# Feed forward up projections of a four layer decoder by one level of Strassen's algorithm, with sums of weights on GpSimd

## The reference

```python
def rms_norm(x, g, eps=RMS_EPS):
    xf = x.astype(jnp.float32)
    y = xf * lax.rsqrt(jnp.mean(xf * xf, axis=-1, keepdims=True) + eps)
    return (y * g.astype(jnp.float32)).astype(x.dtype)

def swiglu(x, w_in, w_out):
    gate, up = jnp.split(x @ w_in, 2, axis=-1)
    return (jax.nn.silu(gate) * up) @ w_out

# per layer:
x = x + mixed
x = x + swiglu(rms_norm(x, W['norm_ffn'][i]), W['ffn_w_in'][i], W['ffn_w_out'][i])
```

## Time and profile before

| | us |
|---|---|
| median of 3 runs | 3497.66 |
| lowest and highest | 3496.62, 3501.85 |
| the profiled execution | 3500.84 |
| its span, first to last instruction | 3499.2 |
| TensorE matmul busy | 3332.0 |
| VectorE busy | 1887.7 |
| ScalarE busy | 1054.7 |
| GpSimd busy | 130.9 |

### The profile page before, as it was taken

How to read it: one execution, slowest core, us unless ns; L and a number is a source line. 1 busy time by engine, 2 the same in 40 slices (tenths; PEclk the granted TensorE clock), 3 DMA queues, 4 the chain that set the end, 5 groups by cost and what they waited for, 6 DMA issues and landing times.

```text
span 3499.2 us, 77068 instructions
## 1 busy us (share of the span) xinstructions
PE 3332.0 (95%) x32788; PEld 3168.7 (91%) x32788; DVE 1887.7 (54%) x2957; ACT 1054.7 (30%) x1674; POOL 130.9 (4%) x247
## 2 busy tenths in 40 slices
PE   8999999998998999988989898899999999899997
PEld 7998899998777999988978777799999999799997
DVE  6667643445655543447457666553344666654343
ACT  3222322223554322223333333332223222232221
POOL 0000000001221000000000000000000000000000
PEclk9999999999999999999999899999999999999998
DMA  3222222223343222221200000122222222122221
GB/s 123 86 80 73 68 85 89 86 94 99 124 126 92 86 95 81 93 89 56 79 17 11 19 11 14 53 87 97 80 97 79 76 78 77 58 91 92 83 91 67
DMA packets 103584, 269.40 MB, mean 77 GB/s; under 512 B 12690, under 2 KB 45714, under 8 KB 103010
## 3 DMA queue, kind: packets, MB, share of 16 engines
q1 hardware_dynamic: 90338, 228.94, 20.1%
q0 software_dynamic: 13056, 37.64, 3.2%
HBM read 248.01 MB, written 18.52 MB: 76 GB/s over the span
## 4 chain that ended last, share of the span: by engine, by line
PE 79%; DVE 11%; DVEq 3%; ACT 3%; issue 2%; SPq 0%; DMA 0%; ACTq 0%
PE ps L559 63%; PE ps L985 4%; PE ps L660 3%; PE ps L977 1%; PE ps L691 1%; PE ps L707 1%; PE ps L1081 1%; DVE cell L2166 1%; DVE arena_r L1873 1%; DVEq L2429 1%; DVE arena L2033 1%; PE ps L685 1%; DVE rstd L1852 1%; DVEq L2165 0%; DVE h L2163 0%
## 5 line engine op out<-in xcount | busy, mean ns | idle before, releaser
L559 PE MATMUL ps<-arena_r 128*128 128x272 f32 x11136 | 1500.5, 293 | 67.4 <-DVE arena_r L2297 21.2
L559 PEld LDWEIGHTS ps<-arena_r 128*128 128x128 f32 x11136 | 1434.4, 191 | 109.0 <-issue 60.7
L559 PE MATMUL ps<-hb_r,arena_r 128*128 128x272 f32 x8448 | 1060.7, 288 | 0.4 <-DVE hb_r L1866 0.4
L559 PEld LDWEIGHTS ps<-hb_r,arena_r 128*128 128x128 f32 x8448 | 1058.5, 188 | 1.1 <-DVE hb_r L1866 0.8
L1368 ACT ACTIVATE arena_r<-ring 128x1024 fp32r<-128x1024 f32 (+1 forms) x240 | 275.3, 1147 | 913.0 <-PE ps L559 913.0
L1892 DVE TENSOR_TENSOR arena_r<-ring,arena_r 128x1024 fp32r<-128x1024 f32 (+1 forms) x240 | 319.6, 1332 | 142.9 <-ACT arena_r L1368 142.9
L1932 DVE TENSOR_TENSOR arena<-ps,rstd 128x544 f32<-128x544 f32 x88 | 63.7, 724 | 292.9 <-PE ps L559 292.9
L1953 DVE TENSOR_TENSOR x<-x,ps 128x544 f32<-128x544 f32 x64 | 46.2, 721 | 293.5 <-PE ps L559 293.5
L1350 ACT ACTIVATE arena_r<-ring 128x1024 fp32r<-128x1024 f32 x80 | 84.6, 1057 | 229.7 <-PE ps L559 224.8
L660 PE MATMUL ps<-arena 128*128 128x128 f32 x1024 | 140.0, 281 | 9.2 <-DVE arena L1996 6.8
L660 PEld LDWEIGHTS ps<-arena 128*128 128x128 f32 x1024 | 128.8, 195 | 13.1 <-issue 7.3
(11 more groups left out here) (387 smaller groups left out, 3099.6 us busy)
## 6 DMA issues: line engine op xcount, KB each, us to landing
ring<-in_w_up SPq DMA_DIRECT2D x176, 512.0 KB, 3.5
ring<-in_w_mix SPq DMA_DIRECT2D x112, 512.0 KB, 3.5
ring<-in_w_down SPq DMA_DIRECT2D x64, 704.0 KB, 4.0
arena<-in_hg_s POOLq DMA_DIRECT2D x16, 512.0 KB, 3.7
out_hg_so<-arena POOLq DMA_DIRECT2D x16, 512.0 KB, 2.9
ring<-in_w_hgout SPq DMA_DIRECT2D x16, 512.0 KB, 3.5
arena<-in_cache_k SPq DMA_DIRECT2D x128, 64.0 KB, 1.9
arena<-in_cache_v POOLq DMA_DIRECT2D x128, 64.0 KB, 2.2
```

The costliest lines, as they stand in the source:

```text
L559: mm = pe.matmul(PS[:, 2 * a + hf, 0:HALF], part[:, ws], rhs[:, o:o + HALF], start=start and n == 0, stop=stop and n == 2)
```

## The change

The gate and linear units of a block are taken as a 2 x 2 matrix of weight blocks: A11 and A12 are the first and second 512 rows of the gate unit, A21 and A22 those of the linear unit. The activations are a 2 x 2 matrix too: first and second half of the features by first and second half of the tokens. Instead of eight products of such blocks there are seven (`NPROD`): A11, S2, S1, S3, A12, A22, S4, in this order. Each has 4 chunks of 3 terms on 272 columns, 12 matmuls. S1 = A21 + A22, S2 = S1 - A11, S3 = A21 - A11 and S4 = S2 - A12 (`sum1` to `sum4`). GpSimd makes the four sums for each pair, from the weights in `ring`, into `ff_s`. The activations' sums T (`ff_t`, `ff_t2` to `ff_t4`, `ff_n1`) are made once for each layer, by GpSimd and VectorE, and split in high and low parts by ScalarE and VectorE.

The seven operands of a pair are split one by one: seven high copies on ScalarE and seven low parts on VectorE, 512 columns each, in five rotating buffers (`ff_operand`, `ff_freed`). The results are combined as the products end. ScalarE copies the product A11 (`ff_e1`); VectorE makes u2, u3 and the four quarters of gate and linear on 272 columns each; `rstd` is multiplied into the two quarters of gate by VectorE and into the whole of linear by GpSimd (`ff_lr`). silu, the product of gate and linear and the split of the result come one pair later. TensorE waits inside a pair three times: before S3 until u2 has read the bank of S2, before A12 until the copy of A11 is made, and before S4 until the second half of linear has read the bank of S1.

21 of the 22 pairs of a layer go this way (`FF_PAIRS` is 10 and 11); the first pair of a layer keeps its 96 matmuls, while the activations' sums are made. The first down unit begins with chunks 8 and 9, and its weights are split in three pieces. SyncE's loads are written out, and the slots of a pair become free when its seven low parts are made. Everything outside the feed forward stays.

```diff
+        NPROD = 7
+        FF_PAIRS = (FU - 1, FU)
...
+        A11, S2, S1, S3, A12, A22, S4 = range(NPROD)
+        WHICH_S = {S1: 0, S2: 1, S3: 2, S4: 3}
+        WHICH_T = {S2: 0, S1: 1, S3: 2, A22: 3}
+        ACCS = (0, 1, 2, 1, 0, 3, 2)
...
+                def pair(s, i, par, first=False):
+                    n0 = NPROD * par
+                    bank = 4 * ((par + 1 - s) % 2)
+                    for k in range(NPROD):
+                        pe.wait_ge(S("ff_wl"), i * (2 * NPROD) + (ff_splits(layer, s) + n0 + k + 1))
+                        if k == S3:
+                            pe.wait_ge(S("ff_u"), i * 6 + (3 * ff_pairs(layer, s) + 3 * par + 1))
+                        if k == A12:
+                            pe.wait_ge(S("ff_e1"), i * 2 + (ff_pairs(layer, s) + par + 1))
+                        if k == S4:
+                            pe.wait_ge(S("ff_u"), i * 6 + (3 * ff_pairs(layer, s) + 3 * par + 2))
+                        wh_, wl_ = ff_operand(s, n0 + k)
+                        begin = k in (A11, S2, S1, A22)
...
+                            hi, lo = token_side(k, c)
+                            for m, (weights, rhs) in enumerate(((wh_, hi), (wh_, lo), (wl_, hi))):
+                                mm = pe.matmul(PS[:, bank + ACCS[k], 0:HALF], weights[:, ws], rhs,
+                                               start=begin and c == 0 and m == 0, stop=c == KC // 2 - 1 and m == 2,
+                                               skip_group_check=True)
+                                if k == S4 and c == KC // 2 - 1 and m == 1:
+                                    mm.then_inc(S("unit_done"), 2)
+                        mm.then_inc(S("ff_p"), 1)
...
+                def first_down(s):
+                    pe.wait_ge(S("ff_x"), 2 * KC * layer + KC * s + 1)
+                    pe.wait_ge(S("ff_g"), FC * layer + FU * s + FU - 1)
+                    for n, c in enumerate((8, 9, 0, 1, 2, 3, 4, 5, 6, 7, 10)):
+                        if n in (0, 2, 6):
+                            pe.wait_ge(S("ff_wl"), ff_downs(layer, s) + (0, 2, 6).index(n) + 1)
+                        pe.wait_ge(S("ff_al"), FC * layer + FU * s + c + 1)
+                        mm = unit_block(2, 0, SLOT, c, ff_ah, ff_al, n == 0, n == FU - 1)
...
-                        for g in range(2):
-                            pe.wait_ge(S("ff_wl"), i * 4 + (unit0 + 2 * par + g + 1))
-                            if begin and not s and par and g:
-                                pe.wait_ge(S("norm_rms"), nth(name) + 1)
-                            first = begin and not s and par == 0
-                            product(2 * par + g, g, ff_hh, ff_hl, KC, "ff_hl" if first and not g else None, KC * layer)
...
+                def pair(s, i, par, begin=False, end=False):
+                    n0 = NPROD * par
+                    weights(s, i, n0 + 4, not (begin and par == 0))
+                    if not (s and begin and par == 0):
+                        silu(s, i, par)
+                    first_product(s, i, par)
...
+                    weights(s, i, n0 + 5)
+                    weights(s, i, n0 + 6)
+                    if not (s and begin and par == 0):
+                        high_a(s, i, par)
+                    if not end:
+                        for k in range(4):
+                            n = n0 + NPROD + k
+                            weights(s, i + n // (2 * NPROD), n % (2 * NPROD))
...
+                    weights(s, i, n0 + 4)
+                    if first and not s:
+                        low_t(3, lambda c: ff_hh[:, c * NT + HALF:(c + 1) * NT],
+                              lambda c: ff_hl[:, c * NT + HALF:(c + 1) * NT], ff_t4)
+                    weights(s, i, n0 + 5)
+                    made(S2)
+                    dve.wait_ge(S("ff_e1"), i * 2 + (ff_pairs(layer, s) + par + 1))
+                    dve.tensor_tensor(ff_u2, b, ff_e1, ALU.add).then_inc(S("ff_u"), 1)
+                    weights(s, i, n0 + 6)
+                    if not (first and s):
+                        glu(s, i, par, not first)
+                    ahead(0)
+                    if not (first and s):
+                        low_a(s, i, par)
+                    made(S3)
+                    dve.tensor_tensor(ff_u3, b, ff_e1, ALU.add)
+                    dve.drain()
+                    dve.tensor_tensor(lin[:, HALF:NT], ff_u3, c, ALU.subtract).then_inc(S("ff_u"), 1)
+                    ahead(1)
+                    made(A12)
+                    dve.tensor_tensor(gate[:, 0:HALF], a, rstd[:, 0:HALF], ALU.mult)
+                    ahead(2)
+                    made(A22)
+                    dve.tensor_tensor(lin[:, 0:HALF], ff_u3, d, ALU.add).then_inc(S("ff_u"), 1)
+                    ahead(3)
+                    made(S4)
+                    dve.tensor_tensor(gate[:, HALF:NT], ff_u2, c, ALU.subtract)
+                    dve.drain()
+                    dve.tensor_tensor(gate[:, HALF:NT], gate[:, HALF:NT], rstd[:, HALF:NT], ALU.mult).then_inc(S("ff_g"), 1)
...
-                        if not first:
-                            ff_rest(layer, i, n + 2, width)
-                        dve.wait_ge(S("unit_done"), i * 4 + (base + n + 2))
-                        dve.tensor_tensor(halves(ff_lin[par]), acc(2 * par + 1), halves(rstd[:, :]), ALU.mult)
-                        if not first:
-                            ff_rest(layer, i, n + 3, width)
-                        dve.drain()
-                        dve.wait_ge(S("ff_silu"), i * 2 + (par + 1 + block0))
-                        dve.tensor_tensor(ff_gate[par], ff_gate[par], ff_lin[par], ALU.mult).then_inc(S("ff_glu"), 1)
...
+                def sum1(s, n):
+                    a11, a12, a21, a22 = raw(s, n)
+                    pool.tensor_tensor(ff_s[0], a21, a22, ALU.add).then_inc(S("ff_s"), 1)
...
+                    pool.tensor_tensor(ff_s[1], ff_s[0], a11, ALU.subtract).then_inc(S("ff_s"), 1)
...
+                    pool.tensor_tensor(ff_s[2], a21, a11, ALU.subtract).then_inc(S("ff_s"), 1)
...
+                    pool.tensor_tensor(ff_s[3], ff_s[1], a12, ALU.subtract).then_inc(S("ff_s"), 1)
+                def pair(s, i, par, end=False):
+                    if not end:
+                        nx, n = par + 1, (par + 1) % 2 * NPROD
+                        arrived(s, i + nx // 2, n)
+                        split(s, i, par, S1)
+                        sum1(s, n)
+                        made(s, i, nx, 1)
+                        sum2(s, n)
+                        split(s, i, par, S3)
+                        sum3(s, n)
+                        made(s, i, nx, 3)
+                        split(s, i, par, S4)
+                        sum4(s, n)
+                    lin = ff_lin[(par + 1 - s) % 2]
+                    pool.wait_ge(S("ff_u"), i * 6 + (3 * ff_pairs(layer, s) + 3 * par + 3))
+                    pool.tensor_tensor(lin, lin, rstd[:, :], ALU.mult).then_inc(S("ff_lr"), 1)
...
```

468 lines of the change are left out of this document (366 added, 102 removed).

## The result

| | us |
|---|---|
| before, median of 4 runs beside it | 3498.72 |
| after, median of 4 runs | 3690.03 (3684.34 to 3693.38) |
| ratio, 95% interval | 1.0544 (1.0526 to 1.0563) |
| the profiled execution after, its span | 3693.38, 3691.8 |

The account below looks back on a forecast made before the run. TensorE bounds the kernel before; VectorE's order, with GpSimd taking turns on SBUF reads, was to bound the changed one. Pairs 136, starts 25, second sets' first pairs 7 and ends 13 add 181 to 3500.84: 3682 us, range 3430 to 3790.

Parts of the forecast that it names:

- Turns on SBUF reads: In the pairs, VectorE operations with two SBUF inputs and GpSimd's reads hold each other back; 3682 us, chance 0.50.
- The signs named: In the trace: low parts over 0.69 us, PSUM readers unchanged, GpSimd sums near 1.2, a pair 13 to 14.5.
- VectorE's own order, 11.0 us: Undisturbed pair: 8.5 us of work, 0.9 and 1.4 idle behind ScalarE, 0.2 register waits; over TensorE's 10.5.
- The pair with turns, 13.7 us: Pair loop: 11.0 plus GpSimd's 6.2 less 3.5 hidden, 1.7 us more than before.
- The start, 6.2 us each: Start of each feed forward, four times: TensorE waits for u2, 3.2 us more, plus 3 for turns.
- Ends, 1.6 us each: End of each set, eight times: TensorE idles before the first down unit, waiting for a low part.
- The first pair of a second set, 1.7 us lost: Four times: this pair gains nothing without disturbance and loses 1.7 us with turns.
- The sum: Whole program with turns: pairs 136, starts 25, second sets' first pairs 7, ends 13, together 181 us, so 3682.
- No disturbance, 3447: Rival for the pairs: GpSimd and VectorE never hold each other back, pair 11.0 us, 54 us faster; chance 0.32.
- VectorE mostly first, 3565: Rival for the pairs: turns, but GpSimd goes into VectorE's free places, pair 12.3 us; chance 0.10.
- The clock: Rival: TensorE's clock falls with its gaps, pair toward 19 to 21 us at half clock; within a shared 0.06.
- rival 1: The same as no disturbance: pairs at 11.0 us, 3447 us in all, range 3405 to 3490; chance 0.32.

Follow-up runs that it names:

- e6: The kernel before, plus five GpSimd sums of 480 columns per pair that nobody reads or waits for; 3502.1 us for 3500.7.
- e1: The changed kernel with GpSimd's five operations in the pair loop on one column, memsets filling the sums' other 511 columns; 3496.4 us, before 3499.2 beside it.
- e3: The changed kernel with GpSimd's five operations in the pair loop on one column each, every wait kept; 3495.4 us, before 3499.2 beside it.
- e9: The changed kernel with sixteen token-side low parts cut to one column at the starts of layers 1 to 3; 3675.9 us for 3690.
- e10: The kernel of e8 with sixteen token-side low parts cut to one column at the starts of layers 1 to 3; 3524.3 us for 3535.6.
- e11: The kernel of e8 with u2 moved forward in the first pair of each feed forward, everything computed; 3531.5 us for 3535.6.
- e7: The changed kernel with only the scaling of linear by rstd moved from GpSimd to VectorE; 3649.6 us, 1.0420 of before.
- e8: The changed kernel without GpSimd arithmetic in pairs: sums on VectorE, rstd applied to down results, product's low part and A11 copy made earlier; 3535.6 us, 1.0100.

## Why the prediction was right, and where its terms were off

**The mechanism.** Turns on SBUF reads: right, by e6 (each holds the other), e1 and e3 (reads, not writes) and the rows by shape. The signs named were there: low parts over 0.69 us, PSUM readers unchanged, GpSimd's sums near 1.2 us alone (1.26 to 1.28; 1.23 was taken from VectorE's 1024 columns), and a pair of 13 to 14.5 us.

**VectorE's own order, 11.0 us.** Right: e3 has 11.1 (11.2 to 11.4 from u2 to u2), and its two waits for ScalarE, 0.93 and 1.44 us, are the 0.9 and 1.4 of the sum. That TensorE's 10.5 would not be reached, even undisturbed, holds.

**The pair with turns, 13.7 us.** From u2 to u2 13.9 to 14.0 in the first set, 13.4 to 13.8 in the second: right in the mean. That 3.5 of GpSimd's 6.2 us would be hidden was a choice; e3's 11.2 to 11.4 from u2 to u2 and 6.4 us of work on GpSimd give 17.6 to 17.8, so 3.8 to 4.0 were.

**The start, 6.2 us each.** The term that was mis-sized: it measures some 12. VectorE's rows there:

```profile
428.38 1.73 DVE L2155 SCALAR_TENSOR_TENSOR arena<-arena,vec 128x272 f32<-128x272 f32 x4
...
430.80 3.53 DVE L2147 TENSOR_TENSOR arena_r<-arena,arena_r 128x272 fp32r<-128x272 f32 x4
...
443.65 1.49 DVE L2147 TENSOR_TENSOR arena_r<-arena,arena_r 128x272 fp32r<-128x272 f32 x4
...
445.66 2.74 DVE L2155 SCALAR_TENSOR_TENSOR arena<-x,vec,arena 128x272 f32<-128x272 f32 x4
...
451.11 0.43 DVE L2207 TENSOR_TENSOR arena<-ps,arena 128x272 f32<-128x272 f32 x1
```

From its first sum (428.38) to u2 (451.11) VectorE needs 22.7 us, nearly without a gap; 19.9 and 3 for turns were counted. The turns are seen too: four low parts take 3.53 us beside GpSimd and 1.49 where it is idle, and the last four sums 2.74 beside it, where the first four took 1.73. Together that is the 3 us. So the work was right and its date was not. The prediction took TensorE's first matmul for the one at 425.47; but its x54 says that 42 of the 96 were already done. The pair begins at 419.86 in the kernel before and at 420.23 after, and VectorE's work starts 8.2 us behind that instead of 1.8. The first u2 comes 30.4 to 30.9 us after the first matmul, where 21.7 and 3 for turns were counted: 6 us late, four times, which makes the term 12. The wait for u2 came out as 4.7 us, 7.7 with turns, and is 11.45. e9, e10 and e11 show that VectorE's work at a start counts nearly in full, wherever u2 stands, as the prediction took it.

**Ends, 1.6 us each.** The wait before the first down unit is 1.7 us (line 654 on 2234): right.

**The first pair of a second set, 1.7 us lost.** Wrong: only ten of a second set's eleven pairs are held up. The first u2 stands 3.1 us behind the last addition of the first set, about the time of 24 matmuls at 0.125 us, and from the last u2 to the next addition it is 17.1 us, as in e3. These 20.2 us are about a pair at TensorE's 10.5, the down unit of 8.3 and the end. So the eleventh pair gains 1.5 us.

**The sum.** Predicted 81 us for four second sets and 99 for four first ones; in the profiled executions they are 62 and 127, together 189 for 181. The first sets are longer than thought by the start, the second ones shorter mainly by the pair that is not held up. Errors of 28 and 19 us, in opposite directions, largely cancel, and that the total comes so near is luck. The profiled executions differ by 192.5 us. The rest is 6.8 us more outside the feed forward less 2 to 3 around the down units. In the executions of e7 and e8, whose mixers are the same, the part outside is no longer than before; so it belongs to the execution, not to the change.

**The rivals.** No disturbance, 3447: e3 shows what it would have been, 3495, hardly a gain. All of the 48 us lie in the first sets. The second ones became 33 us shorter in all, as rival 1 counts them (34); the first ones became 31 us longer, where it has them 21 shorter. Its start term has the same wrong date: the first u2 comes 29.4 to 29.9 us after the first matmul, and 21.7 were counted. That makes 32 us; part of it are GpSimd's sums there, which e3 keeps whole. In the first sets a pair takes 11.3 to 11.4 us instead of 11.0, 13 us more. VectorE mostly first, 3565: not so; e6 shows either first. The clock: TensorE ran at half of it after its long wait, 12 matmuls in 3.06 us. As the pair was VectorE's and not TensorE's, this should cost little; no run separates it.

## What to carry to other kernels

An algorithm that saves an engine's work pays only as far as the next engine has room: here TensorE's work fell by 1.5 us a pair, and VectorE, 45% busy before, got a chain with ScalarE of 11.1 us, which no average showed. "Put it on the idle engine" is wrong where that engine shares a read path with the busy one: a sum of 1.3 us on GpSimd cost more than one of 0.7 on VectorE, though VectorE was the bound. And in a stage whose bound has no slack, whatever is added in front counts nearly in full, so a count at the start belongs beside the gain per step. When a start is dated from a row of the timeline, the row's count tells whether it is the first of its kind: x54 of 96 was not.
